# The recurrence of a hybrid layer: five interleaved lists of work, advanced by a written table of turns

## The chip, the cores and the metric

The kernel runs on one core of one Trainium2 chip. The metric is the device time of one execution in microseconds; for a run on one core that is the time of that core. Engines: TensorE (PE, with its weight loads shown as PEld), VectorE (DVE), ScalarE (ACT), GpSimd (POOL), SyncE (SP, which here only issues DMA).

## The reference

A hybrid layer on 1024 tokens of width 1024, followed by two layers of another kind. Only the first layer matters here. From the normalised input it computes 12 projections of width 1024 and a narrow one. Three branches follow: an RWKV-7 recurrence over 16 heads of 64 channels, a gated depthwise convolution with 31 taps, and attention over 256 memory rows. They are gated, merged and projected.

```
h = rms_norm(x, g_norm);  proj = h @ w_in
r, k, v, w_lo, a_lo = split(token_shift_mix(proj[..., :RWKV_SHIFT], mu_shift))
...
for each token t:                      # state: 64 x 64 per head
    sa    = state @ a_t
    state = state * w_t + sa b_t^T + v_t k_t^T
    y_t   = state @ r_t
wkv = group_norm(y) ...;  o = (wkv + bonus) * silu(rwkv_gate)
...
u = glu_in[:C] * sigmoid(glu_in[C:]);  u = conv_31_taps(u) + b_dw
```

## The kernel before, in words

Channels lie on the 128 partitions, so each of the 8 tiles `ct` holds two heads, and tokens run along the free dimension. The recurrence is solved in 16 chunks of 64 tokens: inside a chunk a triangular system is inverted by doubling (`sx`, `sp`, `sq` at levels 0 to 5), and a chain of 15 small steps (`ch`) carries the state from chunk to chunk.

`build` first writes a `plan`, one list of steps in order. Then each engine's program walks the whole plan and emits its part of each step. So the plan is the order of every engine's queue at once. Each engine works through its queue in order and waits on semaphores where it needs another engine. Nothing else sets the order.

The lists, all Python generators that append steps when advanced:

- `late(ct)`, the solve of tile ct: `G` (four groups of products), `prep`, `vt`, the levels with `ta` and `bt`, `decay`, `w0`, `tu`, `mr`, `ar` of the next tile, `dd`, `bk` of the next tile, `y0`. 24 turns, small matmuls.
- `chain(ct - 1)`, the chain of the tile before: `ch` 1 to 15, `ys`, `gmean`, `gvar`, the group norm on ScalarE and GpSimd (`gnorm`, `gaff`), the sums of the bonus (`bsum`), and the gate projection with `gout`, which multiplies on VectorE and stores tile o.
- `early(ct + 1)`, the next tile's preparation: two `lora` products, the projections k, r and v with their token shift (a copy on ScalarE, then one instruction of VectorE), norms and exponentials up to `powers`. Just before `ar` of the next tile it is run to its end.
- `side()`, 64 side projections: glu_b and glu_a of a tile, then gates g0, g1, g2, q, cg and mg, each followed by a spill: ScalarE copies or takes the sigmoid from PSUM, for cg and mg VectorE multiplies it with PSUM, and a DMA issued by ScalarE stores it.
- `taps(ct)`, the convolution of one tile: 31 instructions of VectorE, each reading two 128x1024 tensors of SBUF. ScalarE's queue holds the issue that stores the tile after the last one. Before glu_a's result is taken, the taps of the tile before are run to their end.

One projection (`P`) is 48 matmuls of 128x512: three products (high by high, low by high, high by low parts), in four turns of twelve. Before each, a weight tile of 512 KB is loaded, copied by ScalarE (w_hi) and its remainder taken by GpSimd (w_lo). A projection and each two-bank sum (`lora`, `ksum`, `bsum`) take a pair of PSUM banks among the lower four (`LOWER`). The small groups take one each of three (`SM`), the chain has the eighth (`YB`). `Slots.take` gives the banks that were taken longest ago and aren't kept; a projection keeps its pair until its last part is planned. TensorE then waits until that pair's previous use has been emptied:

```
first = min((i for i in range(lo, hi, size) if not any(j in kept ...)),
            key=lambda i: max(o for o, _ in self.taken[i:i + size]))
```

Round ct (0 to 8) runs `late(ct)` beside `chain(ct - 1)`. For each turn of `late` the others advance by fixed shares: the chain by one turn, the side projections by 1.0 (1.4 once `early` is through), `early` by one, the taps by 1.5. What is left of the chain is run at the round's end. After the last round come the merge projections `m`, and steps `back_o` and `back_u` that load stored tiles again.

Of the kernel before, what the change touches and what calls it, by code (L numbers as in the profile page):

```python
# [10 lines left out]
NT = 8  # L11
# [143 lines left out]
def run(g):  # L155
    for _ in g:
        pass


def weave(main, *fillers):  # L160
    for share in main:
        for f, n in fillers:
            f.step(n * (share or 1))


def build(nc, ctx, A, out):
# [169 lines left out]
    def do(*step):  # L336
        plan.append(step)

    def P(key, src, h, n=S, m=128, back=False, among=LOWER, deep=2, share=None):


        PROJ[key] = (src, h, n, m, back)
        steps = (n + 511) // 512 * 8 * (1 if h is None else 3)
        deep = deep if h is None else 3 * deep
        for part in range(steps // deep):
            yield share
            if part == 0:
                do("load", key)
                ps.take(("proj", key), 2, among)
                ps.keep(("proj", key), 2)  # L350
            do("proj", key, part * deep, part * deep + deep)
        ps.leave(("proj", key))

    def one(step, use, among):
        ps.take(use, 1, among)
        do(*step)

    def two(step, use, among=LOWER):
        ps.take(use, 2, among)
        do(*step)  # L360
# [3 lines left out]
    def shifted(what, ct, col):  # L364
        yield from P((what, ct), A["w_in"][col], "h", deep=4)
        do("shift", what, ct)

    def between(g, *steps):

        todo = list(steps)  # L370
        for x in g:
            step = todo.pop(0) if todo else None
            if step:
                do(*step)
            yield x

    def early(ct):
        do("lora_load", ct)
        for i in range(2):
            two(("lora", ct, i), ("lora", ct, i))  # L380
            do("lsig", ct, i)
            yield
        do("cs", ct)
        yield from shifted("k", ct, 8 + ct)
        do("ksq", ct)
        yield
        yield
        two(("ksum", ct), ("ksum", ct))
        do("kn", ct)
        yield from between(shifted("r", ct, ct), ("kn2", ct))  # L390
        yield from between(shifted("v", ct, 16 + ct), ("kh", ct), ("rkh", ct))
        yield
        do("powers", ct)

    def bonus(ct):
        two(("bsum", ct), ("bsum", ct))
        do("bon", ct)

    def late(ct):

        for g in range(4):
            for h in range(2):
                ps.take(("G", ct, g, h), 1, SM)
            do("G", ct, g)
            yield
        do("prep", ct)
        for g in range(2):
            one(("vt", ct, g), ("vt", ct, g), SM)
        yield
        for lv in range(6):  # L410
            one(("sx", ct, lv), ("sx", ct, lv), SM)
            do("sxe", ct, lv)
            if lv == 0:
                for g in range(2):
                    one(("ta", ct, g), ("ta", ct, g), SM)
            if lv in (2, 3):
                for g in range(2 * lv - 4, 2 * lv - 2):
                    one(("bt", ct, g), ("bt", ct, g), SM)
            yield
            if lv == 0:  # L420
                continue
            if lv < 5:
                one(("sp", ct, lv), ("sp", ct, lv), SM)
            one(("sq", ct, lv), ("sq", ct, lv), SM)
            do("sqe", ct, lv)
            yield
        do("decay", ct)
        for name, n in (("w0", 2), ("tu", 4), ("mr", 4)):
            for g in range(n):
                one((name, ct, g), (name, ct, g), SM)  # L430
                if g % 2:
                    yield
        if ct + 1 < NT:
            live["ahead"].finish()
            do("ar", ct + 1)
        for g in range(2):
            one(("dd", ct, g), ("dd", ct, g), SM)
        yield
        if ct + 1 < NT:
            do("bk", ct + 1)  # L440
        for g in range(2):
            one(("y0", ct, g), ("y0", ct, g), SM)
        yield
# [4 lines left out]
    def chain(ct):  # L448

        for n in range(1, NCH):  # L450
            one(("ch", ct, n), ("ch", ct, n), YB)
            if ct == 7 and n in COMES_BACK:
                do(*COMES_BACK[n])
            yield
        for g in range(2):
            one(("ys", ct, g), ("ys", ct, g), SM)
        if ct == 7:
            do("back_u", 7)
            for k in (5, 4, 3):
                do("back_o", k)  # L460
        yield
        for c in range(2):
            one(("gmean", ct, c), ("gmean", ct, c), YB if c else SM)
        side_s.take(("gs", ct))
        side_s.keep(("gs", ct), 1)
        do("gsub", ct)
        yield
        yield
        for c in range(2):
            one(("gvar", ct, c), ("gvar", ct, c), YB if c else SM)  # L470
        do("gnorm", ct)
        for k in range(1, 4 if ct == 7 else 1):
            do("uadd", k)
        yield
        do("gaff", ct)
        for k in range(4, 8 if ct == 7 else 4):
            do("uadd", k)
        yield
        while live["ahead"] and live["ahead"].live:
            yield  # L480
        if ct + 2 < NT:
            bonus(ct + 2)
            yield
        yield from P(("gate", ct), A["w_in"][25 + ct], "h", deep=4)
        do("gout", ct)
        side_s.leave(("gs", ct))
        yield

    live = {"taps": None, "ahead": None}

    def taps(ct):
        do("tap", ct, 0)
        for j in range(1, CONV_K):
            yield
            do("tap", ct, j)

    def side():
        todo = [(*x, c_) for c_ in range(NT)
                for x in (("g0", 73), ("g1", 81), ("g2", 89), ("q", 57), ("cg", 49), ("mg", 65))]
        for ct in range(NT):  # L500
            yield from P(("glu_b", ct), A["w_in"][41 + ct], "h", deep=4)
            side_s.take(("glu", ct))
            side_s.keep(("glu", ct), 1)
            do("glu_s", ct)
            yield from P(("glu_a", ct), A["w_in"][33 + ct], "h", deep=4)
            if live["taps"]:
                live["taps"].finish()
            do("glu", ct)
            side_s.leave(("glu", ct))
            live["taps"] = Filler(taps(ct))  # L510
            for kind, col, c_ in todo[5 * ct:5 * ct + 5] if ct < 7 else todo[35:]:
                yield from P((kind, c_), A["w_in"][col + c_], "h", deep=4)
                side_s.take((kind, c_))
                do("spill", kind, c_)
        live["taps"].finish()
# [39 lines left out]
    ps.leave(("stat", "x"))  # L555
    run(shifted("lo", 0, 24))
    do("lo_tanh")
    other = Filler(side())
    weave(early(0), (other, 1.0))
    do("ar", 0)  # L560
    do("bk", 0)
    bonus(0)
    other.step(2)
    for ct in range(NT + 1):
        states = Filler(chain(ct - 1) if ct else iter(()))
        ahead = live["ahead"] = Filler(early(ct + 1) if ct + 1 < NT else iter(()))
        if ct < NT:
            do("eye", ct)
        for _ in late(ct) if ct < NT else range(21):
            states.step()  # L570
            other.step(1.0 if ahead.live else 1.4)
            ahead.step()
            if live["taps"]:
                live["taps"].step(1.5)
        if ct == 0:
            bonus(1)
        states.finish()
    other.finish()


    BACK = (7, 6, 5, 4, 3, 0, 2, 1)
# [83 lines left out]
    ahead = Filler(conv_norm())  # L665
    weave(merge(0, "w_proj_rwkv", None), (ahead, 0.55))
    ahead.finish()
    ahead = Filler(memory())
# [2402 lines left out]
```

## Time and profile before

| | |
|---|---|
| time, median of 3 runs | 4130.01 us (4125.48 to 4137.75) |
| the profiled execution, time | 4137.17 us |
| its span, first to last instruction | 4135.2 us |
| busy share of PE, PEld, DVE, ACT, POOL | 91%, 56%, 46%, 35%, 24% |
| mean granted clock of TensorE | 0.954 |

The span is one profiled execution. An engine's busy share is the union of its instructions over the span. The first `G` step of tile 0 begins at 158 us. The last side projection ends at 1767 us, and the first merge projection begins at 1769 us. Tile 1's first `G` begins at 345 us, tile 2's at 533, tile 3's at 739, tile 4's at 924, tile 5's at 1108, tile 6's at 1301 and tile 7's at 1490. The granted clock is given as a share of full speed. 1.0 is 2.4 GHz and 0.5 is 1.2 GHz.

### The profile page before, as it was taken

How to read it: one execution, taken by the hardware profiler on the slowest of the kernel's cores; microseconds unless marked ns; L12 is line 12 of the kernel's file. 1: busy time of each engine (PE TensorE's matmuls, PEld its weight loads, DVE VectorE, ACT ScalarE, POOL GpSimd, SP SyncE). 2: the span in 40 equal slices, each digit the busy share in tenths (PEclk: the TensorE clock that was granted, in tenths of full speed). 3: DMA queues.
4: the chain of work that ended last, by engine and by line, in shares of the span. 5: the costliest groups of instructions: out<-in, count | busy, mean ns of one | idle time of the engine just before them, and what ended most of it. 6: DMA issues, size and time to landing. Idle time of an engine off the chain costs nothing.

```text
span 4135.2 us, 76284 instructions
## 1 busy us (share of the span) xinstructions
PE 3751.5 (91%) x34076; PEld 2304.6 (56%) x34076; DVE 1899.4 (46%) x2057; ACT 1453.2 (35%) x1831; POOL 997.1 (24%) x438
## 2 busy tenths in 40 slices
PE   6998999999999999999899897997979888998977
PEld 3565656666665666546545455655555455655544
DVE  3456454645545464352332426436362345445352
ACT  4223222232313222231222334554543344544542
POOL 2423232333323242212134221111111310111102
PEclk9999999999999999999999998999989998998989
DMA  2111111111111111333231120010102201101102
GB/s 100 52 38 42 48 47 43 42 56 44 58 37 58 37 60 63 140 122 132 97 128 62 68 63 28 21 51 16 48 12 84 73 27 32 37 31 32 42 35 79
DMA packets 64695, 235.94 MB, mean 57 GB/s; under 512 B 7856, under 2 KB 9584, under 8 KB 63856
## 3 DMA queue, kind: packets, MB, share of 16 engines
q1 hardware_dynamic: 55296, 198.03, 14.3%
q10 hardware_dynamic: 9072, 33.03, 2.0%
q8 instruction: 268, 4.39, 0.4%
q14 instruction: 59, 0.48, 0.0%
HBM read 174.93 MB, written 47.71 MB: 54 GB/s over the span
## 4 chain that ended last, share of the span: by engine, by line
PE 73%; DVE 14%; ACT 6%; DMA 2%; issue 2%; POOL 1%; SPq 1%; DVEq 0%; ACTq 0%; POOLq 0%
PE psum L1036 71%; DVE arena L2165 6%; DVE arena L2168 4%; ACT arena L1620 4%; PE psum L1039 2%; DVE arena L2634 1%; ACT wh L1620 1%; DMA arena<-in_w_proj_conv 1%; DVE arena L2570 1%; POOL hl L2693 1%; SPq L2896 1%; DMA arena<-arena 1%; DMA arena<-in_w_in 1%; ACT arena L2099 1%; DVE arena L2172 0%
## 5 line engine op out<-in xcount | busy, mean ns | idle before, releaser
L1036 PE MATMUL psum<-arena 64*64 64x32 f32 (+12 forms) x23404 | 1349.9, 253 | 228.6 <-DVE arena L2165 106.0
L1036 PEld LDWEIGHTS psum<-arena 64*64 64x64 f32 (+8 forms) x23404 | 982.5, 139 | 617.7 <-issue 329.6
L2693 POOL TENSOR_TENSOR wl<-arena,wh 128x1024 bf16<-128x1024 f32 (+1 forms) x203 | 497.8, 2452 | 2144.3 <-ACT wh L1620 2141.2
L1036 PE MATMUL psum<-hh,wh 128*128 128x512 f32 x3248 | 902.0, 421 | 76.3 <-ACT hh L1620 27.9
L1036 PE MATMUL psum<-hh,wl 128*128 128x512 bf16 x3248 | 827.8, 396 | 1.6 <-POOL wl L2693 1.6
L1620 ACT ACTIVATE arena<-psum 128x512 f32<-128x512 f32 (+4 forms) x660 | 416.2, 631 | 1118.3 <-PE psum L1036 790.4
L1036 PE MATMUL psum<-hl,wh 128*128 128x512 bf16 x3248 | 768.7, 383 | 8.0 <-POOL hl L2693 8.0
L1036 PEld LDWEIGHTS psum<-hh,wh 128*128 128x128 f32 x3248 | 609.9, 193 | 281.4 <-issue 50.2
L2168 DVE SCALAR_TENSOR_TENSOR arena<-arena 128x1024 f32<-128x1024 f32 x356 | 581.8, 1634 | 211.6 <-ACT arena L1620 197.9
L2165 DVE TENSOR_TENSOR arena<-psum,arena 128x512 f32<-128x512 f32 (+3 forms) x456 | 280.1, 614 | 715.8 <-PE psum L1036 500.4
L2165 DVE TENSOR_TENSOR arena<-arena 128x512 f32<-128x512 f32 (+9 forms) x494 | 404.0, 818 | 399.9 <-DMA arena<-arena 184.0
L2693 POOL TENSOR_TENSOR arena<-arena 128x1024 f32<-128x1024 f32 (+4 forms) x142 | 364.9, 2570 | 820.9 <-ACT arena L1620 456.5
L1036 PEld LDWEIGHTS psum<-hl,wh 128*128 128x128 bf16 x3248 | 312.8, 98 | 396.2 <-issue 30.6
L1036 PEld LDWEIGHTS psum<-hh,wl 128*128 128x128 bf16 x3248 | 287.5, 98 | 430.4 <-issue 110.7
L1620 ACT ACTIVATE wh<-arena 128x1024 fp32r<-128x1024 f32 (+1 forms) x203 | 213.6, 1052 | 799.4 <-PE psum L1036 637.3
L1620 ACT ACTIVATE arena<-arena 128x1024 f32<-128x1024 f32 (+4 forms) x378 | 347.2, 919 | 347.3 <-DVE arena L2165 145.1
L2168 DVE SCALAR_TENSOR_TENSOR arena<-psum,arena 128x1024 f32<-128x1024 f32 (+2 forms) x73 | 83.2, 1140 | 385.3 <-ACT arena L1620 224.6
L2634 DVE TENSOR_REDUCE arena<-psum 128x1 f32<-128x1024 f32 x128 | 156.8, 1225 | 124.5 <-PE psum L1036 115.7
L2099 ACT ACTIVATE arena<-psum,arena 128x1024 f32<-128x1024 f32 x128 | 142.8, 1115 | 183.1 <-DVE arena L2634 174.6
L1039 PE MATMUL psum<-arena 128*128 128x128 f32 x928 | 144.4, 299 | 46.9 <-ACT arena L2099 21.9
L1039 PEld LDWEIGHTS psum<-arena 128*128 128x128 f32 x928 | 117.5, 153 | 81.9 <-ACT arena L2099 27.6
L1620 ACT ACTIVATE arena<-psum,arena 128x1024 f32<-128x1024 f32 (+1 forms) x98 | 102.5, 1046 | 121.7 <-PE psum L1036 117.4
(38 smaller groups left out, 775.4 us busy)
## 6 DMA issues: line engine op xcount, KB each, us to landing
arena<-in_w_in SPq DMA_DIRECT2D x161, 512.0 KB, 3.6
scr_g<-arena ACTq DMA_DIRECT2D x24, 512.0 KB, 2.6
arena<-scr_g SPq DMA_DIRECT2D x24, 512.0 KB, 4.4
arena<-in_w_out SPq DMA_DIRECT2D x24, 512.0 KB, 3.5
arena<-in_w_mem_kv SPq DMA_DIRECT2D x16, 512.0 KB, 3.5
scr_x<-arena SPq DMA_DIRECT2D x16, 512.0 KB, 3.6
arena<-arena SPq DMA_DIRECT2D x64, 128.0 KB, 2.3
arena<-scr_x SPq DMA_DIRECT2D x16, 512.0 KB, 7.1
```

The source lines that it names most:

```text
L1036: return pe.e.matmul(o, l, r, start=start, stop=stop)
L1039: return pe.e.matmul(o, i, ident if idn is None else idn, start=True, stop=True, is_transpose=True)
L1620: return act.seq.activation(o, i, func, bias=bias, scale=scale)
L2099: act.seq.activation(EX[z] if c == 0 else EX[2], pair(use), AF.Exp, bias=s[:, c:c + 1], scale=-1.0, accum_out=s[:, 4 + c:5 + c]).then_inc( ...
L2165: return dve.seq.tensor_tensor(o, a, b, op)
L2168: return dve.seq.scalar_tensor_tensor(o, a, s, b, op0, op1)
L2570: dve.seq.copy_predicated(AT8(p, g), m, i).then_inc(*dve.up("ATl", *use))
L2634: dve.seq.tensor_reduce(s[:, c:c + 1], pair(use), AX.X, MIN).then_inc(*dve.up("dmax", L, h, q, c))
L2693: return pool.seq.tensor_tensor(o, a, b, op)
L2896: sp.e.dma_start(SWAP[a], PX[b]).then_inc(*(sp.land("swapped", L, h, i) if j == 3 else sp.land("swapped", L, h, i, j)))
```

## The change

The fixed shares go. A table `ROUNDS` has one string for each of the nine rounds. Each letter is one turn of one list: l for `late`, c for `chain`, e for `early`, s for the side projections, t for a tap. A letter whose list has ended does nothing. After a string, what is left of `late` and of the chain is run, and after the last one what is left of the side projections. The steps inside the lists, their number, the bank rule and the runs to the end inside `late` and `side` are as before.

```diff
@@ -555,27 +555,54 @@
     ps.leave(("stat", "x"))
     run(shifted("lo", 0, 24))
     do("lo_tanh")
-    other = Filler(side())
+    others = side()
+    other = Filler(others)
     weave(early(0), (other, 1.0))
     do("ar", 0)
     do("bk", 0)
     bonus(0)
     other.step(2)
-    for ct in range(NT + 1):
-        states = Filler(chain(ct - 1) if ct else iter(()))
-        ahead = live["ahead"] = Filler(early(ct + 1) if ct + 1 < NT else iter(()))
-        if ct < NT:
-            do("eye", ct)
-        for _ in late(ct) if ct < NT else range(21):
-            states.step()
-            other.step(1.0 if ahead.live else 1.4)
-            ahead.step()
-            if live["taps"]:
-                live["taps"].step(1.5)
-        if ct == 0:
-            bonus(1)
-        states.finish()
-    other.finish()
+    ROUNDS = (
+        "lcsetlsettlsetlsettlseltsettlsetletsltelsettlsetlsetttlsetlsetettlsetstettlsllsttttttstleltstlssttls"
+        "tlsttl",
+        "slcsetlcetstlcselctelcselseclcelscescssletlcsetclstlscetetlcetslctseslttcssetltcetlsltcseecslctsttcl"
+        "stlssctttlsctlctsccclc",
+        "tlstetlcetsclcsetlcteslcetstlcetslcetctlsstetlcesclesltctttselcsetlctetlctselctseltstlccstelesetclts"
+        "scslclltlsccsscscclcc",
+        "slcsettlsectlcsetlctetlcsttelcslceetlcsstetlcsetltseltctsetctlcsetlcstcesscletlelttctslcseetcttletsc"
+        "lsttstlcscsslclslcccclsc",
+        "llscelcslcesetlcsttectselsecttlsectlsctettlcselctselcestlcsttstcelcetlecsttlcettllsltctecsseltetstlc"
+        "ssctstlcsstcltlcsttccclc",
+        "slcselcsltceselcslceelecslctsetltcesltcsettlcseltcsetclsettlcsttlecssectlsesttltcecletlcttlessctlsct"
+        "ctslcsstttlllcsttccscc",
+        "slcsetlcestlctslceelcselseclcslceslescsetlcsettclstclsetetlctsetlcsecttlssteltcellstcetsettcscslltsc"
+        "stlcsstctltlctsclccc",
+        "tlcsettslcstlcstlcsstlctlssctltcslscslcsttstclssltslcscttlcstlctssltcclsstttslstlcstlsccltcstsslttlt"
+        "stcctlsctsclcc",
+        "csttcsstcttecstsscstcstcsscscsctsscscssscscsccssccssscscsscccccssssc",)
+
+    def rounds(others):
+        for ct in range(NT + 1):
+            ahead = live["ahead"] = Filler(early(ct + 1)) if ct + 1 < NT else None
+            lists = dict(l=late(ct) if ct < NT else iter(()), c=chain(ct - 1) if ct else iter(()), s=others)
+            if ct < NT:
+                do("eye", ct)
+            for x in ROUNDS[ct]:
+                if x == "t":
+                    if live["taps"]:
+                        live["taps"].step()
+                elif x == "e":
+                    if ahead:
+                        ahead.step()
+                else:
+                    next(lists[x], None)
+            run(lists["l"])
+            if ct == 0:
+                bonus(1)
+            run(lists["c"])
+
+    rounds(others)
+    run(others)
 
 
     BACK = (7, 6, 5, 4, 3, 0, 2, 1)
```

## Rows read from the trace of the kernel before

**Rows 1.** The page: busy time by engine, and the chain that ended last.

```profile
PE 3751.5 (91%) x34076; PEld 2304.6 (56%) x34076; DVE 1899.4 (46%) x2057; ACT 1453.2 (35%) x1831; POOL 997.1 (24%) x438
...
PE 73%; DVE 14%; ACT 6%; DMA 2%; issue 2%; POOL 1%; SPq 1%; DVEq 0%; ACTq 0%; POOLq 0%
```

**Rows 2.** Windows: length, busy us of PE, PEld, DVE, ACT, POOL, clock, DMA.

```profile
158.00:1770.00 1612.00, 1551.97 (x17290) 1005.12 (x17291) 855.20 (x802) 445.16 (x537) 504.77 (x235) 0.98 0.16 54
1770.00:4135.20 2365.20, 2086.87 (x16355) 1241.19 (x16353) 995.19 (x1221) 948.32 (x1239) 445.71 (x180) 0.94 0.17 58
```

**Rows 3.** TensorE's waits from 158 to 1770 us: total, times, longest.

```profile
PE psum L1036 <- DVE arena L2165: 47.2, 25, 6.7
PE psum L1036 <- ACT arena L1620: 15.6, 7, 8.7
PE psum L1036 <- DVE arena L2168: 1.4, 1, 1.4
```

**Rows 4.** Timeline of TensorE: start, length, instructions, idle time before and who ended it.

```profile
231.69 4.60 PE L1036 MATMUL psum<-hh,wh 128*128 128x512 f32 x12 [2.53 <-DVE arena L2165]
...
313.54 1.97 PE L1036 MATMUL psum<-arena 64*64 64x128 f32 x16 [8.71 <-ACT arena L1620]
345.01 2.49 PE L1036 MATMUL psum<-arena 64*128 64x128 f32 x20 [6.73 <-DVE arena L2165]
...
417.80 3.02 PE L1036 MATMUL psum<-hh,wh 128*128 128x512 f32 x12 [1.16 <-ACT arena L1620]
...
543.50 5.89 PE L1036 MATMUL psum<-arena 64*128 64x512 f32 x24 [6.11 <-DVE arena L2165]
...
659.99 3.89 PE L1036 MATMUL psum<-arena 64*64 64x32 f32 x68 [3.58 <-DVE arena L2165]
...
1308.87 5.72 PE L1036 MATMUL psum<-arena 64*128 64x512 f32 x24 [4.01 <-DVE arena L2165]
...
1671.71 0.33 PE L1036 MATMUL psum<-arena 64*64 64x64 f32 x4 [2.15 <-DVE arena L2165]
...
1769.04 3.27 PE L1036 MATMUL psum<-arena 128*128 128x512 f32 x7 [2.42 <-DVE arena L2165]
```

**Rows 5.** Timeline of VectorE and ScalarE around 300 us.

```profile
298.00 9.21 DVE L2168 SCALAR_TENSOR_TENSOR arena<-arena 128x1024 f32<-128x1024 f32 x7
...
307.25 0.33 ACTq L1863 DMA_DIRECT2D scr_cu<-arena  x1
...
312.28 2.50 ACT L1620 ACTIVATE arena<-psum 128x256 f32<-128x256 f32 x6
```

**Rows 6.** Timeline of GpSimd and VectorE before 345 us.

```profile
335.39 6.40 POOL L2693 TENSOR_TENSOR arena<-arena 64x1024 f32<-64x1024 f32 x2 [0.17 <-POOL wl L2693]
...
339.73 5.14 DVE L2165 TENSOR_TENSOR arena<-arena 64x1024 f32<-64x1024 f32 x2
```

**Rows 7.** Timeline of the end of gate 0: ScalarE, then VectorE.

```profile
534.50 1.28 ACT L1627 ACT_TABLE_LOAD   x1
535.79 1.02 ACT L1620 ACTIVATE arena<-psum 128x1024 f32<-128x1024 f32 x1
...
538.11 2.10 DVE L2165 TENSOR_TENSOR arena<-arena 128x1024 f32<-128x1024 f32 x1
```

**Rows 8.** Windows at clock 0.50: one of ten, and the sum of the ten.

```profile
542.80:553.00 10.20, 9.50 (x33) 6.47 (x34) 7.00 (x7) 2.17 (x2) 2.38 (x1) 0.50 0.14 54
...
sum 61.90, PE 48.41 PEld 32.64 DVE 47.05 ACT 15.36 POOL 20.01; mean PE 4.84 PEld 3.26 DVE 4.70 ACT 1.54 POOL 2.00
```

**Rows 9.** Timeline: a projection's part at low clock, and two taps beside GpSimd.

```profile
549.32 4.72 PE L1036 MATMUL psum<-hh,wh 128*128 128x512 f32 x12
...
561.09 8.05 DVE L2168 SCALAR_TENSOR_TENSOR arena<-arena 128x1024 f32<-128x1024 f32 x2
```

**Rows 10.** Groups by form, 158 to 1770 us: count, busy, mean ns.

```profile
L2168 DVE SCALAR_TENSOR_TENSOR arena<-arena 128x1024 f32<-128x1024 f32 x261 | 440.1, 1686 | 25.2 <-ACT arena L1620 16.1
...
L2165 DVE TENSOR_TENSOR arena<-psum,arena 128x512 f32<-128x512 f32 x192 | 132.8, 692 | 219.4 <-PE psum L1036 204.8 <-POOL arena L2747 4.4 <-DVE arena L2165 0.5
```

## The prediction

> **What bounds the kernel now.** I read the page's totals and its chain of waits first [rows 1]: TensorE is busy for 91% of the span and carries 73% of the chain that ended last; VectorE has 14%. Then busy time by stretch [rows 2]. The recurrence and what runs beside it, the only place that the change touches, is the stretch from 158 to 1770 us, and there TensorE is busy for 1551.97 of 1612 us. The 2365 us behind it hold the same instructions in the same order after the change. So the question is the 60.0 us in which TensorE is idle there, and the clock. The view of TensorE's waits [rows 3] says who ends them: 33 waits with 64.2 us, 4.58 of them in front of the first turn, so 59.6 that a new order can reach; 48.6 end on VectorE, 15.6 on ScalarE. Last come the waits one by one [rows 4] and the windows in which the granted clock was 0.50 of full [rows 8]. None ends on a transfer.
>
> **The change removes and adds no work.** I advanced the five lists by hand rules, first as the old loop does, then by the letters of the table: both give the same 1654 steps (matmul groups, evictions, DMA issues). Every queue, SyncE's and GpSimd's too, holds the same instructions, in its part of the new order, and ScalarE has 50 table loads by either. What changes is which work of TensorE lies between a matmul group and the next one that needs what the first leaves behind: its PSUM bank, or its result by way of VectorE or ScalarE. I call that work the cover, and add it up with 2.8 us for twelve projection matmuls, 1.9 for a solve step of 64 instructions, 1 for a group of the rest.
>
> **Term 1, banks taken with no cover.** A projection or a two-bank sum takes the pair of banks that was taken longest ago. The old loop ends a projection and its spill and at once takes something else, and at eleven places that is the pair just written: cover 0. All eleven wait, 1.1 to 1.2 us where ScalarE empties the pair by one copy (417.80 is one), 1.4 where VectorE does, 2.4 to 2.5 where VectorE multiplies behind the copy (231.69), 4.0 and 6.1 where two more products of VectorE stand in front (1308.87, 543.50) [rows 4]. The table parts nine of them: r of tile 1 gets 6.6 us of cover, the second lora product of tile 2 gets 1.4, cg 1 gets 16, the first of tile 3 gets 3.9 (its pair is now the one that gate 0 left, a copy and a product ago), k 4 gets 1.4, the second of tile 6 gets 1.4, r 6 gets 6.8, mg 4 gets 17, the first of tile 7 gets 7.0. Each cover is at least the time that such a pair took to be emptied, so the nine waits go: 2.53 + 1.11 + 1.38 + 6.11 + 1.11 + 1.21 + 1.16 + 2.42 + 4.01 = **21.0 us** (the first at 231.69, the last at 1308.87). Two stay as they are.
>
> **Term 2, two long waits of tile 0.** At 313.54 the second `mr` group waits 8.71 us for ScalarE. It needs the bank of `tu` 2, whose eviction stands on ScalarE behind the issue that stores the convolution's tile, and that waits for seven taps in a row, 9.21 us, begun at 298.00 [rows 5]. From the end of the projection v to this `mr` the old order has 10.4 us of cover, the new one 17.1. The other side is a copy of 1.1, the shift 1.3, seven taps 9.2, a solve addition 0.7, the issue 0.3 and the eviction 1.3: 13.9 us. Too little before, enough after: 8.7 us. At 345.01 the first `G` of tile 1 waits 6.73 us for `bk`, 5.14 us on VectorE from 339.73, beside 6.40 on GpSimd [rows 6]. In the old order VectorE reaches `ar` only after the product of spill mg 0, which waits for that projection. The new one has `ar` ahead of it and 2.8 us more cover; counted from the last `mr`, VectorE has two taps 2.6, `ar` 1.2 and 3.2, then waits for mg 0 (at 10.5), the copy and product 2.3, a tap 1.3, `bk` 5.1: 19.2, and `G` comes at 19.8. 6.7 us. Together **15.4 us**.
>
> **Term 3, the last solve level.** Seven waits, 8.3 us in all, stand in front of `sx` level 5 (659.99 is the longest, 3.58 [rows 4]): the level's addition is behind the shift of r, `kh` and taps. The new order gives 8.5 to 11.8 us of cover instead of 5.6 to 5.9 at tiles 0, 1, 5, moves `kh` ahead at tile 3, and has one tap fewer at tile 2: 0.54 + 0.39 + 1.71 + 1.47 + 1.3 = **5.4 us**.
>
> **Term 4, the end.** The first merge projection takes the pair of mg 7, just written, and waits 2.42 us (1769.04 [rows 4]). In the new order gate 7 comes before mg 7, so its pair is the older one: **2.4 us**. In the last round the wait of 2.15 us at 1671.71 goes, but chain step 4 now follows step 3 with two taps and no cover, which I price the same: 0.
>
> **Term 5, new waits.** I counted every bank that is taken again with under 2.95 us of cover: 25 before, 57 after. Of the 25, eleven are those of cover 0. The other fourteen had 1.4 to 2.8 us and waited 0.78 + 2.15 us in all, 0.21 each. After, five have 0 to 0.3 (two old, `G` 1 of tile 4, the pair of g1 1 for g2 1, chain step 4), and 52 have 1.1 to 2.9: at 0.21 each 10.9 us, 8.0 more than now. A mask product, the eviction of a `G` bank, takes 0.69 [rows 10]. `G` 1 of tile 4 follows `G` 0 at once and needs its first bank, emptied behind the gate product of the chain; the same chain once ran from the table load at 534.50 to 540.21 [rows 7], begun 1.2 us after its projection. So the bank comes 5.5 (1.28 + 1.02 + 1.23 + 1.23 + 0.69, the durations at their least) to 7.6 us after it, against 3.9 of cover: 1.6 to 3.7, I take 2.7. g2 1 pays 0.9, a copy's 1.16 less its cover. **Minus 11.6 us.** Bounds: 4 if the 38 more short covers cost nothing, 45 if each waits 1.1 us.
>
> **Term 6, the clock.** In ten stretches, 61.9 us, the clock was 0.50 of full, which is the level of 1.2 GHz, and each began at or right behind a wait; TensorE was busy for 48.41 us of them [rows 8]. Twelve matmuls of 128x512 took 3.02 us at full clock (417.80 [rows 4]) and 4.72 at 549.32, where the clock came back at 553.0 [rows 9]. So 1.04 us at full speed did 4 and 3.68 us did 8 of them, 0.47 against 0.25 us each: a busy microsecond at the low level loses 0.46. Seven stretches lie behind waits that go, with 32.1 busy us (9.50 of them at 542.8 [rows 8]): 14.8 us. Three new ones of 3.4 us behind new waits take 4.7. **10.1 us**; bounds 0 and 22.
>
> **Sum.** 21.0 + 15.4 + 5.4 + 2.4 − 11.6 + 10.1 = 42.7 us. The profiled execution took 4137.2 us (span 4135.2), 7.2 above the median of the three runs, inside their spread of 12.3. Off its own time that is 4094.5; off the median of 4130.0 it is 4087.3. I predict **4088 us**.
>
> **Rivals.** *The short covers wait.* If each of the 38 waits as the eleven of cover 0 do, (21.0 + 1.16 + 1.16) / 11 = 2.1 us, they cost 80 us and the other new ones 3.6, against 44.2 removed and 10.1 of clock: slower by 29, 4159 us. It decides once their mean passes (44.2 + 10.1 − 3.6) / 38 = 1.3 us. For it: VectorE is one queue, and a tap of 1.3 us can stand in front of any eviction. Against it: the 0.21 us of the fourteen places at hand. Chance 0.09. The Trainium skill (Perfetto Trace Analysis, Matmuls) has independent matmul groups rotate through banks so that the emptying of one overlaps the next; by the count alone the new order rotates worse, and the rule would choose this rival, but the trace agrees only for covers near 0.
>
> *Waits move within VectorE's queue.* A tap takes 1.32 us in the burst at 298.00 [rows 5] and 1.69 in the mean over 261 instructions of its form [rows 10]; two took 8.05 us at 561.09, while GpSimd was at work [rows 9]. If the new places of the taps meet GpSimd more often, say 16 of the 248 by 2.7 us (8.05 / 2 − 1.32), VectorE has 43 us more. It is busy for 855 of 1612 us [rows 2] and so isn't the bound, but half of that ahead of evictions that TensorE waits for takes 22 us: 4110. Chance 0.18 for this and other gains of 12 to 25 us. The Trainium skill (GPSIMD Engine Reference, Specifications) says that GpSimd shares its SBUF interfaces with VectorE and collides with instructions of two SBUF inputs, as taps are; by it only the order relative to GpSimd counts, and the trace agrees.
>
> *Nothing comes of it.* The waits are replaced one for one. With new waits near 1 us (38 + 3.6) and no clock gained, 2.6 us are left: 4127. Chance 0.15.
>
> **Numbers.** The forecast case, a gain of 25 to 60 us, has 0.58. Faster by over 0.3% (12.4 us, about what a measurement of this kernel tells from no change) is 0.58 + 0.18 and 0.01 of the third case: 0.77; within 0.3% the rest of it, 0.14; slower 0.09. Likeliest case: 4070 to 4105. The range, from all bounds of terms 5 and 6 in favour (44.2 − 4 + 22 = 62, so 4068) to the third case: **4068 to 4126**.
>
> **What would show it.** TensorE's idle time in the recurrence falls from 60 to about 27 us; none of the waits at 313.54, 345.01, 543.50 and 1308.87 has a counterpart over 2 us; windows at clock 0.50 add up to under 30 us; busy time of VectorE, ScalarE and GpSimd is within 3% of now, and the part behind 1770 us keeps its 2365 us within 5. Term 5 is wrong if waits under 2 us add up to more than 20; the whole is wrong if a long wait arises where I saw none, above all at `G` 1 of tile 4 or where `powers` now stands in front of an eviction on ScalarE.

## The result, and the profile after

The kernel with the table takes 4062.97 us in the median of four runs (4055.27 to 4066.35), the one before, measured beside it, 4132.93 (4125.48 to 4137.75). The ratio is 0.9831, with a 95% interval of 0.9812 to 0.9850: 70 us faster, where I had forecast 43, and 5 us below the lower end of my range.

The page of the profiled execution (time 4055.27 us, span 4053.4, mean granted clock 0.966), busy time by engine and the chain that ended last, against [rows 1]:

```profile
PE 3711.4 (92%) x34076; PEld 2281.7 (56%) x34076; DVE 1874.0 (46%) x2057; ACT 1454.2 (36%) x1831; POOL 986.9 (24%) x438
...
PE 76%; DVE 12%; ACT 5%; DMA 2%; issue 2%; POOL 1%; SPq 1%; DVEq 0%; ACTq 0%; POOLq 0%
```

Every count of instructions is the same as before. TensorE has 40 us less busy time with the same matmuls, and its mean granted clock went from 0.954 to 0.966. VectorE's part of the chain has shrunk by two points.

The windows that answer to [rows 2], cut at the same two places of the program:

```profile
158.00:1704.50 1546.50, 1529.34 (x17291) 992.51 (x17292) 829.51 (x801) 445.23 (x537) 495.77 (x235) 0.99 0.16 56
1704.50:4053.40 2348.90, 2067.69 (x16355) 1230.59 (x16353) 996.28 (x1222) 949.16 (x1240) 445.36 (x180) 0.95 0.17 58
```

The recurrence is 65.5 us shorter. Of that 42.9 us is idle time of TensorE (60.0 before, 17.2 now) and 22.6 is its busy time (1551.97 before, 1529.34 now). The part behind it, which is the same program, is 16.3 us shorter too, with 19.2 less busy time at a clock of 0.95 instead of 0.94. I don't count this to the change. In the profiled executions of all twelve kernels told of here that part took 2350 to 2366 us, with its busy time going along, and the one before stands at the upper end and the one after at the lower. The medians say the same: the profiled execution of before was 4 us above its median and that of after 8 us below.

TensorE's waits in the first window, against [rows 3]:

```profile
PE psum L1063 <- DVE arena L2192: 15.6, 11, 4.6
PE psum L1063 <- ACT arena L1647: 4.6, 5, 1.2
PE psum L1063 <- DVE arena L2195: 0.4, 1, 0.4
```

17 waits instead of 33, and 20.6 us instead of 64.2. The longest, 4.6, is the one ahead of the first `G`. Of the others none is longer than 1.7 us. The timeline of TensorE at the places of [rows 4] and at the new waits:

```profile
172.31 0.69 PE L1063 MATMUL psum<-arena 64*128 64x512 f32 x2 [1.16 <-ACT arena L1647]
...
288.97 1.20 PE L1063 MATMUL psum<-arena 64*64 64x128 f32 x18 [1.70 <-DVE arena L2192]
...
296.23 3.71 PE L1063 MATMUL psum<-arena 64*64 64x128 f32 x64
...
324.49 1.42 PE L1063 MATMUL psum<-arena 64*128 64x128 f32 x20
...
374.78 1.43 PE L1063 MATMUL psum<-hh,wh 128*128 128x512 f32 x5 [0.90 <-ACT arena L1647]
...
516.44 3.01 PE L1063 MATMUL psum<-hh,wh 128*128 128x512 f32 x12 [1.59 <-DVE arena L2192]
519.38 1.98 PE L1063 MATMUL psum<-arena 64*128 64x512 f32 x4
522.70 3.27 PE L1063 MATMUL psum<-arena 64*128 64x128 f32 x21 [1.34 <-DVE arena L2192]
...
887.16 1.16 PE L1063 MATMUL psum<-arena 64*128 64x128 f32 x16 [0.89 <-DVE arena L2192]
...
1203.15 1.09 PE L1063 MATMUL psum<-arena 64*64 64x128 f32 x16 [0.87 <-ACT arena L1647]
...
1703.51 1.02 PE L1063 MATMUL psum<-arena 128*128 128x512 f32 x2
```

The row at 296.23 has the last `tu` groups of tile 0 and its first two `mr` groups with nothing idle between them, so the 8.71 us ahead of the second are gone. The row at 324.49 begins with the first `G` of tile 1, without the 6.73 us that it waited at 345.01. The one at 519.38 is `lora` of tile 3, without its 6.11. The one at 1703.51 is the first merge projection, without its 2.42. The row at 374.78 is g2 1 and that at 887.16 is the second `G` of tile 4, two of the new waits that I had named. Of the windows at clock 0.50 two are left in the recurrence, against the ten of [rows 8] and one at its start:

```profile
157.90:164.70 6.80, 5.60 (x25) 3.11 (x26) 4.94 (x5) 0.00 (x0) 5.26 (x3) 0.50 0.22 81
523.10:533.30 10.20, 10.20 (x33) 4.68 (x31) 6.48 (x7) 2.45 (x3) 1.26 (x1) 0.50 0.17 54
```

The second begins behind the waits of 1.59 and 1.34 us at 516.44 and 522.70.

### The profile page after: what moved, and what is told of

Same layout as the page of the kernel before. It is cut to its first block, busy times and chain, and to the rows that moved or that the text cites. A ratio compares the mean times of both kernels' runs of the same rounds, so it can differ in the third digit from the quotient of the medians.

```text
span 4053.4 us, 76293 instructions
## 1 busy us (share of the span) xinstructions
PE 3711.4 (92%) x34076; PEld 2281.7 (56%) x34076; DVE 1874.0 (46%) x2057; ACT 1454.2 (36%) x1831; POOL 986.9 (24%) x438
## 4 chain that ended last, share of the span: by engine, by line
PE 76%; DVE 12%; ACT 5%; DMA 2%; issue 2%; POOL 1%; SPq 1%; DVEq 0%; ACTq 0%; POOLq 0%
PE psum L1063 74%; DVE arena L2192 6%; ACT arena L1647 3%; DVE arena L2195 3%; PE psum L1066 2%; DVE arena L2661 1%; DMA arena<-in_w_proj_conv 1%; DVE arena L2597 1%; ACT wh L1647 1%; POOL hl L2720 1%; SPq L2923 1%; DMA arena<-arena 1%; ACT arena L2126 1%; POOL arena L2720 0%; DMA arena<-in_w_in 0%
## 5 line engine op out<-in xcount | busy, mean ns | idle before, releaser
L1063 PE MATMUL psum<-arena 64*64 64x32 f32 (+12 forms) x23404 | 1329.7, 251 | 188.8 <-DVE arena L2192 76.5
L1063 PEld LDWEIGHTS psum<-arena 64*64 64x64 f32 (+8 forms) x23404 | 967.6, 138 | 569.9 <-issue 317.3
L1063 PE MATMUL psum<-hh,wh 128*128 128x512 f32 x3248 | 889.3, 417 | 73.4 <-ACT hh L1647 27.9
L2195 DVE SCALAR_TENSOR_TENSOR arena<-arena 128x1024 f32<-128x1024 f32 x356 | 557.7, 1567 | 205.1 <-ACT arena L1647 191.3
L2720 POOL TENSOR_TENSOR arena<-arena 128x1024 f32<-128x1024 f32 (+4 forms) x142 | 354.7, 2498 | 835.1 <-ACT arena L1647 453.2
L2661 DVE TENSOR_REDUCE arena<-psum 128x1 f32<-128x1024 f32 x128 | 156.8, 1225 | 120.5 <-PE psum L1063 111.5
L1066 PE MATMUL psum<-arena 128*128 128x128 f32 x928 | 144.7, 300 | 47.9 <-ACT arena L2126 22.6
```

Source lines behind the costliest of these rows:

```text
L1063: return pe.e.matmul(o, l, r, start=start, stop=stop)
L1066: return pe.e.matmul(o, i, ident if idn is None else idn, start=True, stop=True, is_transpose=True)
L2195: return dve.seq.scalar_tensor_tensor(o, a, s, b, op0, op1)
L2661: dve.seq.tensor_reduce(s[:, c:c + 1], pair(use), AX.X, MIN).then_inc(*dve.up("dmax", L, h, q, c))
L2720: return pool.seq.tensor_tensor(o, a, b, op)
```

## The experiments

One table holds the readings, so that each experiment can be read against the others. "Time" is the median in us, with the ratio to the kernel before, measured beside it. "Recurrence" is the profiled execution from the first instruction of the first `G` to that of the first merge projection. "Idle" is that length less TensorE's busy time in it, "busy low" is TensorE's busy time in its windows at clock 0.50, and "VectorE" is the busy time of that engine in the recurrence. The recurrence has the same instructions in each.

| kernel | time | ratio (95%) | recurrence | busy | idle | busy low | VectorE |
|---|---|---|---|---|---|---|---|
| before | 4132.9 | | 1610.8 | 1551.0 | 59.8 | 53.7 | 855.0 |
| after | 4063.0 | 0.983 (0.981 to 0.985) | 1544.4 | 1528.4 | 16.1 | 15.9 | 828.5 |
| e1 | 4116.2 | 0.996 (0.995 to 0.997) | 1596.5 | 1552.1 | 44.4 | 58.0 | 849.8 |
| e2 | 4086.8 | 0.989 (0.986 to 0.991) | 1564.6 | 1531.7 | 32.9 | 21.0 | 834.3 |
| e3 | 4074.9 | 0.986 (0.984 to 0.988) | 1557.8 | 1532.3 | 25.5 | 25.5 | 834.6 |
| e4 | 4140.4 | 1.003 (1.001 to 1.004) | 1618.7 | 1553.8 | 64.9 | 60.9 | 831.6 |
| e5 | 4100.7 | 0.992 (0.990 to 0.993) | 1585.2 | 1547.6 | 37.6 | 49.7 | 854.1 |
| e6 | 4081.9 | 0.987 (0.986 to 0.989) | 1564.1 | 1538.2 | 25.9 | 31.0 | 848.4 |
| e7 | 4061.9 | 0.983 (0.981 to 0.984) | 1541.0 | 1528.0 | 13.0 | 16.0 | 828.5 |
| e8 | 4043.2 | 0.978 (0.977 to 0.980) | 1534.9 | 1522.0 | 12.9 | 3.1 | 828.5 |
| e9 | 4061.1 | 0.984 (0.982 to 0.986) | 1544.9 | 1528.7 | 16.3 | 16.5 | 828.6 |
| e10 | 4094.9 | 0.992 (0.989 to 0.995) | 1582.2 | 1544.6 | 37.5 | 43.5 | 854.0 |

### e1 and e2: the table by rounds

The old shares can be written as letters, and then one kernel can have the new row for round 0 and old rows for the rest (e1), or the reverse (e2):

```diff
# e1: new row 0 (with one s and one t more, so that the counts are the old ones), old rows 1 to 8
-        "tlsttl",
-        "slcsetlcetstlcselctelcselseclcelscescssletlcsetclstlscetetlcetslctseslttcssetltcetlsltcseecslctsttcl"
-        "stlssctttlsctlctsccclc",
+        "tlsttlst",
+        "lcsetlcsettlcsetlcsettlcsetlcsettlcsetlcsettlcsetlcsettlcsetlcsettlcsetlcsettlcsetlcselcselcselcsslc"
+        "slcsstlcsttlcstl",
...
# e2: the old row 0 (one s and one t less, for the same reason), new rows 1 to 8
-        "lcsetlsettlsetlsettlseltsettlsetletsltelsettlsetlsetttlsetlsetettlsetstettlsllsttttttstleltstlssttls"
-        "tlsttl",
+        "lsetlsettlsetlsettlsetlsettlsetlsettlsetlsettlsetlsettlsetlsettlsetlsettlsetlsetlsttlstlssttlstltl",
```

Expected of e1:

> The table's first string alone; the other eight rounds carry the old loop's order, written as strings (two letters are added at the end of round 0 so that round 1 begins in the old state). Cover theory (the gain is TensorE's order around banks that were taken again with no cover, and the clock follows long waits): the waits 2.53, 8.71, 6.73 and 0.54 of tile 0 go, 1.70 comes (the first tu behind w0, as in the changed kernel), minus 17 us, and three stretches at half clock with 10.5 busy us go, minus 5: 22 below before, about 4111. Tap theory (the gain is the taps' new places, VectorE having 26 us less of busy time in the changed kernel): one round of eight, 9 below, about 4124.

Expected of e2:

> The counterpart: the old order in round 0, the table in the other eight. Cover theory: 22 us above the changed kernel, about 4085. Tap theory: 9 above it, about 4072. If the two halves don't add up to the whole gain of 70, the rounds are not independent.

Measured: e1 takes 4116.2 us and e2 4086.8, beside 4130.9 for the kernel before. The recurrence gets shorter by 14.3 us in e1 and by 46.2 in e2, together 60.5 of the 66.4 of both. So about a quarter of the gain lies in round 0 and three quarters in the other eight rounds. e1 lies 5 us above the 4111 of the cover theory and 8 below the 4124 of the tap theory, e2 2 above the 4085 of the first and 15 above the 4072 of the second. In e2 TensorE's timeline still has the two waits of tile 0, and in e1 the 6.1 us ahead of tile 3's `lora`; e2 first, then e1:

```profile
309.53 1.97 PE L1062 MATMUL psum<-arena 64*64 64x128 f32 x16 [8.70 <-ACT arena L1646]
...
341.14 2.48 PE L1062 MATMUL psum<-arena 64*128 64x128 f32 x20 [6.74 <-DVE arena L2191]
```

```profile
525.58 4.80 PE L1063 MATMUL psum<-arena 64*128 64x512 f32 x14 [6.10 <-DVE arena L2192]
```

Each wait is thus made, and taken away, by the order of its own round. That is term 2 of the forecast, 15.4 us, to a tenth: 8.70 + 6.74. Round 0 of the table takes 15.4 us of idle time in e1 as well (59.8 less 44.4), after it has brought waits of its own of 1.92 us (`tu` of tile 0) and 1.50 us (the first lora product of tile 2).

The 5 us of clock that I expected of e1 did not come. Its busy time at half clock is 58.0 us, 4 more than before. Three of its short waits were each followed by a stretch at 0.50: 1.50 us at 329.44, 1.47 at 830.63 and 1.34 at 1560.49. The last two are in the kernel before as well, 1.47 us at 849.70 and 1.35 at 1576.40, and none of its ten stretches lies behind them. The windows of e1 behind the first and the third:

```profile
330.90:337.70 6.80, 6.80 (x30) 3.48 (x29) 5.50 (x8) 1.11 (x1) 0.00 (x0) 0.50 0.00 1
1563.20:1570.00 6.80, 6.80 (x57) 3.87 (x54) 4.18 (x5) 0.00 (x0) 0.95 (x1) 0.50 0.01 2
```

The reverse occurs too: the 2.53 us ahead of r of tile 1, at 229.25 in e2, were followed by no stretch at 0.50, and the same wait before, at 231.69, was.

### e3 and e4: the places of the taps alone

e3 has the table's order of everything but the taps, and after each turn of `late` as many taps as the old loop makes there. e4 is the reverse. Row 0 of e3:

```diff
-        "lcsetlsettlsetlsettlseltsettlsetletsltelsettlsetlsetttlsetlsetettlsetstettlsllsttttttstleltstlssttls"
-        "tlsttl",
+        "lcsetlsettlsetlsettlsetlsettlsetlesttletlsettlsetlsettlsetlseettlsesetlsttltlsstlettlstlssttlstlsttl",
...
```

Expected of e3:

> The table's letters l, c, e and s as they are, but the taps where the old loop had them, counted by the turns of late (of the chain in the last round). TensorE's order is that of the changed kernel. Cover theory: at most 10 us above the changed kernel, 4063 to 4073. Tap theory: most of the gain is lost, 4100 or more, and VectorE's busy time in the recurrence is back near 855 us.

Expected of e4:

> The counterpart: the old order of l, c, e and s, taps where the table has them. TensorE's order is that of the kernel before, with its eleven pairs of cover 0. Cover theory: within 10 us of before, 4120 to 4133. Tap theory: 4098 or less, VectorE's busy time near 829 us.

Measured: e3 takes 4074.9 us, 12 more than the whole table; e4 takes 4140.4, 10 more than before. e3 is 2 us above the upper end of the cover theory and 25 below the 4100 of the tap theory. e4 is 7 us above the upper end of the first and 42 above the 4098 of the second. VectorE's busy time doesn't follow the times. Its groups by form in the recurrence, for e4 and then for the kernel after, against the first row of [rows 10]:

```profile
L2195 DVE SCALAR_TENSOR_TENSOR arena<-arena 128x1024 f32<-128x1024 f32 x261 | 419.4, 1607 | 25.2 <-ACT arena L1647 16.1
```

```profile
L2195 DVE SCALAR_TENSOR_TENSOR arena<-arena 128x1024 f32<-128x1024 f32 x261 | 416.0, 1594 | 25.2 <-ACT arena L1647 16.1
```

In the table's places the 261 taps take 416.0 us instead of 440.1. In each of these traces a tap beside which GpSimd is idle takes 1.28 to 1.29 us, and 59 taps take over 2 us before, 46 in e4 and 44 after: fewer meet GpSimd. e4 has nearly all of that (419.4) and is slower than the kernel before. So a shorter VectorE is worth nothing here by itself, and that theory falls. (e3 alone couldn't have shown it: its VectorE is busy for 834.6 us, not for the 855 that the tap theory wanted.) What counts is which eviction has a tap in front of it. In e4 the fourth `mr` group of tile 4 waits 5.60 us at 1072.88, where it waited 0.99 before. The instructions of VectorE that it waits for stand behind three taps, where one of 1.29 us stood:

```profile
1065.93 5.89 DVE L2195 SCALAR_TENSOR_TENSOR arena<-arena 128x1024 f32<-128x1024 f32 x3
1071.95 1.87 DVE L2192 TENSOR_TENSOR arena<-psum,arena 128x256 f32<-128x256 f32 x4
```

In e3 five waits of 1.8 to 4.1 us stand in the timeline, and the kernel after has none over 1.7. One of them, chain step 5 of tile 3, on TensorE and then on VectorE:

```profile
920.68 0.48 PE L1062 MATMUL psum<-arena 64*64 64x64 f32 x4 [4.02 <-DVE arena L2191]
```

```profile
912.82 2.92 DVE L2199 TENSOR_SCALAR arena<-arena 128x1024 f32<-128x1024 f32 x1
915.78 4.51 DVE L2194 SCALAR_TENSOR_TENSOR arena<-arena 128x1024 f32<-128x1024 f32 x1
```

The same stretch of VectorE in the kernel after:

```profile
907.19 2.92 DVE L2200 TENSOR_SCALAR arena<-arena 128x1024 f32<-128x1024 f32 x1
910.21 0.23 DVE L2192 TENSOR_TENSOR arena<-psum,arena 128x64 f32<-128x64 f32 x1
910.47 7.51 DVE L2195 SCALAR_TENSOR_TENSOR arena<-arena 128x1024 f32<-128x1024 f32 x2
```

Here the chain's addition of 0.23 us stands ahead of the slow taps, there a tap of 4.51 us stands ahead of it, in both cases while GpSimd runs two products, 6.4 us together. And at each of the five waits, or right behind it, a stretch of half clock begins; three of them:

```profile
299.10:302.50 3.40, 3.30 (x19) 2.74 (x20) 2.28 (x3) 3.21 (x6) 0.00 (x0) 0.51 0.17 65
...
729.20:736.00 6.80, 6.36 (x47) 5.28 (x48) 6.45 (x7) 1.19 (x2) 6.52 (x4) 0.50 0.19 74
920.40:923.80 3.40, 3.12 (x10) 1.77 (x11) 2.58 (x3) 0.00 (x0) 3.19 (x3) 0.50 0.09 19
```

So with the 9.4 us of idle time that e3 has more, its recurrence is 13.4 us longer, and that answers to the measured 12.

### e5, e6 and e7: the bank rule instead of the order

If term 1 is right, its waits must go without any new order, by choosing another pair. The rule takes the pair that was taken longest ago, but a projection holds its pair for 48 matmuls, and other pairs are taken meanwhile. So at its end its pair is often the oldest by that count, and just written. In these three the pair gets its date when the projection's last part is planned, in the recurrence alone. e5 has the old order, e6 the rounds of e1, e7 the whole table.

```diff
     def leave(self, use):
+        if self.by_end:
+            self.order += 1
+            for j in self.kept[use]:
+                if self.taken[j][1] == use:
+                    self.taken[j] = (self.order, use)
         del self.kept[use]
...
+    ps.by_end = True
     rounds(others)
     run(others)
+    ps.by_end = False
```

Expected of e5:

> The order of the kernel before, every list's turns as they were; only the choice of a pair of banks changes, within the recurrence: the pair whose last use was planned to its end longest ago, not the pair taken longest ago. That removes all eleven places of cover 0 (their cover becomes 2.8 to 8.4 us) and the pair of mg 7 in front of the first merge projection. If these places carry the gain: waits minus 23.4 and 2.4, four stretches at half clock with 21.6 busy us gone, minus 10, so about 36 below before, 4095. If the gain needs the steps themselves moved (the interleaving of solve, chain and projections), this is within 10 us of before.

Expected of e6:

> As the last, with the table's first string as well. If the nine pairs and tile 0's two waits are the whole cause, their sum: 36 and the 15 that the first string alone gave (less the 2.5 us of r 1, counted in both), 48 below before, 4083, and what is left to the changed kernel's 4063 is the solve level's waits and the clock. If the pairs don't matter, 4116 as with the first string alone.

Expected of e7:

> The changed kernel with that choice of banks in the recurrence. It has three places of cover 0 to 0.3 left at pairs (the second lora product of tile 1, r 2, g2 1), which waited 1.16, 1.16 and 0.90 us: 3 us below the changed kernel, 4060, if nothing else moves; more than 5 above it if the table fits the old choice alone.

Measured: 4100.7, 4081.9 and 4061.9 us beside 4134.2 for the kernel before. In e5 the idle time falls by 22.2 us (59.8 to 37.6). The eleven waits of cover 0 are 23.4 us and the one ahead of the first merge projection 2.4. Nine of the eleven are gone and that one too; the first lora product of tile 3 still waits 0.75 us and mg 4 0.94, and two new waits of 1.07 and 0.90 us have come. The long waits of tile 0 stay where they were:

```profile
307.93 1.97 PE L1070 MATMUL psum<-arena 64*64 64x128 f32 x16 [8.72 <-ACT arena L1654]
...
340.56 2.49 PE L1070 MATMUL psum<-arena 64*128 64x128 f32 x20 [6.74 <-DVE arena L2199]
```

So the mechanism of term 1 is shown. In the traces the recurrence is 25.6 us shorter in e5, 3.4 us of it busy time, where I had expected 10 from the clock; the medians differ by 33, and that difference I can't place. By the medians the rule alone gives 33 us with the old order, 34 with round 0 of the table (e1 to e6), and with the whole table 1, which is nothing beside the spread of the runs: the table's order had already parted nine of the eleven pairs. In e7's trace the waits of the other two and of g2 1 are gone, 3.0 us of idle time. The order and the rule take the same waits, and only the rest of the table, 38.8 us from e5 to e7 (44.1 in the traces' recurrence), is the order's alone.

### e8, e9 and e10: the rule elsewhere

The rule can hold ahead of and behind the recurrence too. e8 has it everywhere with the table, e9 behind the recurrence only, e10 everywhere with the old order.

```diff
# e8 and e10, in place of the switches around rounds():
         self.kept = {}
+        self.by_end = True
# e9:
     rounds(others)
     run(others)
+    ps.by_end = True
```

Expected of e8:

> The same with the choice of banks by the planned end in the whole kernel, the two other layers too, where TensorE idled some 255 us. Those stages hold their pairs over whole uses and take them in turn, so I expect 4055 to 4065; 20 or more below the changed kernel if they too re-take pairs just written.

Expected of e9:

> The new order of turns, with the rule that takes the pair whose last use ended longest ago applied only behind the recurrence. With the rule everywhere the time was 4043.15 us, with the rule in the recurrence alone 4061.91, without it 4062.97. If the 19 us between the first two come from the part behind the recurrence, where waits that end on an eviction were some 10 us shorter in the profile, this one takes 4045 to 4055 us, and its part behind the recurrence is 8 to 15 us shorter than in the kernel without the rule. If they come from the part ahead of the recurrence (3 us less idle there) and from the clock in the recurrence, it takes 4058 to 4063.

Expected of e10:

> The old order of turns, with the rule that takes the pair whose last use ended longest ago applied everywhere. With the rule in the recurrence alone the old order took 4100.72 us. If the further gain of the rule elsewhere (19 us with the new order) doesn't hang on the order of turns, this one takes 4078 to 4086 us, and its distance to the new order with the rule everywhere (4043.15) stays at some 39 us. If that gain came about only together with the new order, it takes 4095 to 4101.

Measured: e8 takes 4043.2 us, the fastest of all and 20 below the kernel after; e9 takes 4061.1, so the rule behind the recurrence brings nothing that shows; e10 takes 4094.9, 6 below e5. But e10 and e5 were measured beside the kernel before at different times, when that one took 4126.8 and 4134.2 us, and their ratios to it are the same 0.992. So with the old order no gain from the rule elsewhere is shown. The windows of e8 up to the first `G` and in the recurrence, then that of e7 up to the first `G`:

```profile
0.00:154.67 154.67, 112.82 (x433) 57.56 (x433) 49.43 (x36) 59.74 (x55) 46.86 (x24) 0.94 0.24 84
...
154.67:1689.53 1534.86, 1522.00 (x17288) 989.78 (x17289) 828.45 (x800) 444.05 (x536) 494.43 (x235) 1.00 0.16 56
```

```profile
0.00:159.63 159.63, 114.88 (x432) 59.11 (x433) 49.25 (x36) 59.73 (x55) 46.81 (x24) 0.92 0.23 82
```

The first `G` comes at 154.67 and in e10 at 153.86, against 156.8 to 159.6 in the ten kernels without the rule there. That is 2 to 6 us. In the recurrence another 6.2 go, 6.0 of it busy time: e8 has the same idle time as e7 and the same waits, 1.58 us at 507.17 and 1.33 at 513.43, but no half clock behind them (busy low 3.1 instead of 16.0). The part behind, 2350.8 against 2357.5, gives the other 6.7, within what it varies by. So of the 19 us between e7 and e8 two to six are the rule's, ahead of the recurrence. How much of the others hangs on where the clock happens to fall, and would stand in other executions, is left open. With the old order the recurrence's share was 3.0 us (e5 to e10).

## Why the forecast was too small

The direction, the places and the mechanisms of terms 1 to 4 held. The gain of the recurrence, 66.4 us (1610.8 less 1544.4), against the 42.7 of the sum, term by term:

| term | forecast | measured |
|---|---|---|
| 1, nine pairs of cover 0 | 21.0 | 21.0, none has a counterpart |
| 2, tile 0 | 15.4 | 15.4, none has a counterpart |
| 3, waits ahead of `sx` level 5 | 5.4 | 8.3, all seven |
| 4, first merge projection | 2.4 | 2.4 |
| waits that I left in place | 0 | 9.1 |
| 5, new waits | −11.6 | −12.9 |
| 6, clock | 10.1 | 22.7 |
| sum | 42.7 | 66.0 |

The measured column sums the waits that one timeline has and the other hasn't; for the clock it is the fall of TensorE's busy time with the same instructions.

**Term 6 was mis-sized, and it carries half of the miss.** I let three of the ten stretches stay and three new ones come. None of the ten was left, and one new one came, at 523.1, behind two new waits: busy time at half clock outside the start fell from 48.4 to 10.2 us, by 38, where the forecast's seven less three stretches make 22 (32.1 less 4.7 / 0.46). The rate was low too. 22.7 us of busy time went with 37.8 busy us at half clock, 0.60 each, and over the twelve kernels of the table the length is 1519.5 + idle + 0.57 × busy low to within 1.7 us; I had taken 0.46 from one pair of groups, which gives 17.4 for the 37.8. So of the 12.6 us that term 6 lacks, 7.3 are stretches that I left in and 5.3 the rate. The Trainium skill (TensorE: Matmul & The Clock Gate, HAM oscillation — how this bites in real kernels) counts half of the throttled time as lost. By that, the windows at 0.50 here, 67.0 us in the recurrence before and 15.9 after, make an estimate of 25.6 us, half of the 51.1 between them: nearer to the measured 22.7 than my 17.4 is. Why the rate per busy microsecond lies above one half I didn't find out.

Two of the three stretches that I let stay lie behind waits that I had left in place (1.95 at 569.98 and 2.15 at 1671.71), the third behind the 3.58 at 659.99, of which I had counted 1.3 as saved. All three waits were gone or under 0.5 us. Of thirteen new waits, none longer than 1.7 us, only the two at 516.44 and 522.70 have a stretch behind them, and in e8 not even they. That no more came can't be credited to a rule: in e1 single waits of 1.34 to 1.50 us did bring one, and in e2 the wait of 1.34 at 1376.74 did too, which in the kernel after, at 1360.19, did not. So a charge for new waits wasn't a mistake in kind; its size here is partly luck.

**Waits left in place.** Nine small waits that I didn't treat, 0.3 to 2.15 us each, were gone too, or nearly: 1.95 ahead of `vt` of tile 2, 1.35, 0.99, 0.85 and smaller ones, and the 2.15 of the last chain, whose place I had priced as taken by another of the same size; that one is 0.47. Together with the rest of term 3 that is 12.0 us. It is also why the range was too narrow: its lower end took "all bounds in favour" of terms 5 and 6, but none for terms 1 to 4, as if a wait that I couldn't explain away had to stay.

**Term 5 had the right size for the wrong reason.** Of the 38 more short covers only two waited, `tu` and `y0` of tile 5, 0.87 and 0.53 us: 0.04 us each, not 0.21. The second `G` of tile 4, priced at 2.7, waited 0.88 at 887.16; g2 1 waited its 0.90. The other 9.2 us lie outside the short covers, most of them where I counted 4 us and more: 1.70 at 288.97 (`tu` of tile 0), 1.59 and 1.34 around 520, and five of 0.4 to 1.3. The first of them on VectorE:

```profile
283.97 4.15 DVE L2195 SCALAR_TENSOR_TENSOR arena<-arena 128x1024 f32<-128x1024 f32 x2
288.23 0.69 DVE L2192 TENSOR_TENSOR arena<-psum,arena 128x512 f32<-128x512 f32 x1
```

The addition of 0.69 us, of the last solve level, for which `tu` waits stands behind two taps of 4.15 us together. It is VectorE's queue in front of the eviction that is late, and the count of cover on TensorE doesn't see that.

**The rivals.** The short covers don't wait: what the Trainium skill (Perfetto Trace Analysis, Matmuls) asks for, that groups rotate so that an eviction overlaps the next one, is met with 1.1 us between them, and e5 shows what it costs where there is none. That the taps collide with GpSimd more often was wrong in sign, 24 us less instead of more, and e4 shows that this total wouldn't have decided anything. That nothing comes of it is refuted by the result.

**The signs.** Idle time in the recurrence fell to 16 us, further than the 27 that I gave, and no long wait arose. The windows at 0.50 add up to 15.9 us, under 30. Two signs failed: VectorE's busy time in the recurrence fell by 3.1%, not within 3, and the part behind it is 16 us shorter in these two profiles, not within 5, which its variation over the twelve kernels covers.

## What to carry to other kernels

When one engine is busy for 96% of a stretch, its idle time can be read off wait by wait, and each wait is the matter of two queues: what that engine does in between, and what stands in front of the eviction on the other. A buffer that is held for long should be dated by the end of its last use, not by when it was taken: a few lines gave 33 us here by the medians, 26 of them seen in the recurrence, without touching the order. And the half clock is best priced as a whole, by the busy time that it covers, not wait by wait: here nearly all of it went with the waits above 1.7 us, but the same short wait had a stretch behind it in one kernel and none in another.

## What the runs showed of the hardware

The granted clock falls at short waits: at or behind 1.82, 2.33 and 3.45 us in e3 came 3.4 us at 0.50 each, behind single waits of 1.50 and 1.34 us in e1 6.8 us each, and in the kernel after behind two waits of 1.59 and 1.34 us, 4.9 us of work between them, 10.2 us. The same two waits in e8 were followed by none, and so was one of 2.53 us in e2, so they can't be priced singly. A tap of two SBUF inputs that took 1.3 us alone took up to 4.5 beside products of GpSimd; over the 261 taps the table made that 24 us less, and e4, with 21 us of it and no gain, shows that no time came of it.
